# Softmax attentions with two output banks, index scores among slabs, and a residual loaded piece by piece

## The reference

```python
# block 1
h = rms_norm(x); z = h @ w_in                    # glu, q, k, v, two gates
a = silu(rms_norm(causal_depthwise_conv(glu, 31 taps))); y_a = a @ w_conv_out
q, k = rms_norm per head                          # 16 heads of 64
o = sum over 3 dilation groups of softmax(q k' - slope * dist) v   # one merged softmax
y_b = o @ w_attn_out
x = x + (sigmoid(gate_a) * y_a + sigmoid(gate_b) * y_b) @ w_out
x = x + (silu(u_gate) * u_val) @ w_down           # u = 3-tap conv(rms_norm(x) @ w_up)
# layer A: attention over the 128 best keys of an index
score = sum_h relu(qi_h . ki) * wi_h              # 8 index heads
p = softmax(rope(q) rope(k)' over top 128 of score);  y = (p v * silu(g)) @ w_out_a
x = layer_norm(ALPHA * x + y)
# layer B: stick-breaking attention, gate, w_out_b, layer_norm; its result is the output
```

## Time and profile before

| | us |
|---|---|
| median of 3 runs | 1651.69 |
| lowest, highest | 1646.33, 1653.17 |
| the profiled execution | 1649.88 |
| its span | 1648.10 |
| mean granted TensorE clock | 0.984 |

### The profile page before, as it was taken

The page is one execution under the profiler, slowest core; times in us unless marked ns, Lnnn a source line. Parts: engine busy times, 40 slices in busy tenths (PEclk is TensorE's granted clock), DMA queues, the critical chain, the costliest instruction groups (busy, mean ns, idle before and its releaser), DMA issues.

```text
span 1648.1 us, 19418 instructions
## 1 busy us (share of the span) xinstructions
PE 1561.9 (95%) x7634; PEld 1273.9 (77%) x7634; DVE 886.0 (54%) x1546; ACT 504.5 (31%) x1001; POOL 546.1 (33%) x662
## 2 busy tenths in 40 slices
PE   6999999899899999999999999999998989999997
PEld 5878888677778778888878787687776768888885
DVE  2899949256645144333400031895676261677675
ACT  4223333356541132222200011311676130444440
POOL 3222234311114344444444444144110334332321
PEclk9999999999999999999999999999999999999999
DMA  8989998623338978898888888398321758755655
GB/s 227 193 184 194 195 191 188 153 66 63 77 77 183 225 169 193 191 198 190 196 172 192 184 176 194 78 189 182 77 52 26 164 120 193 156 123 117 140 109 145
DMA packets 69274, 253.12 MB, mean 154 GB/s; under 512 B 7616, under 2 KB 7744, under 8 KB 69184
## 3 DMA queue, kind: packets, MB, share of 16 engines
q0 software_dynamic: 66528, 242.25, 68.7%
q1 hardware_dynamic: 2112, 7.53, 1.3%
q10 hardware_dynamic: 544, 2.10, 0.4%
HBM read 249.75 MB, written 2.10 MB: 153 GB/s over the span
## 4 chain that ended last, share of the span: by engine, by line
PE 86%; DVE 5%; DMA 3%; ACT 3%; issue 2%; POOL 0%; SPq 0%; DVEq 0%; ACTq 0%; POOLq 0%
PE PSUM L451 26%; PE PSUM L452 25%; PE PSUM L453 25%; DMA W_LO<-wstream 2%; PE PSUM L612 2%; PE PSUM L633 2%; PE PSUM L714 1%; PE PSUM L732 1%; PE PSUM L745 1%; PE PSUM L600 1%; DVE MASK L1747 1%; DMA SMALLS<-small 1%; DMA W_HI<-wstream 1%; PE PSUM L643 1%; ACT PROBS L968 0%
## 5 line engine op out<-in xcount | busy, mean ns | idle before, releaser
L439 POOL DMA_DIRECT2D W_HI<-wstream x231 | 129.5, 561 | 946.8 <-PE PSUM L453 946.3
L451 PE MATMUL PSUM<-X_HI,W_HI 128*128 128x512 f32 x872 | 350.0, 401 | 5.7 <-DVE X_LO L1332 2.6
L452 PE MATMUL PSUM<-X_LO,W_HI 128*128 128x512 f32 x872 | 342.1, 392 | 0.0
L453 PE MATMUL PSUM<-X_HI,W_LO 128*128 128x512 f32 x872 | 342.0, 392 | 0.0
L433 POOL DMA_DIRECT2D W_LO<-wstream x231 | 208.0, 900 | 105.2 <-POOL W_LO L430 84.2
L451 PE MATMUL PSUM<-W_HI,X_HI 128*128 128x512 f32 x544 | 213.8, 393 | 7.0 <-DMA W_LO<-wstream 2.7
L430 POOL TENSOR_SCALAR W_LO<-W_HI 128x1024 fp32r<-128x1024 f32 x195 | 210.3, 1079 | 23.1 <-DMA W_HI<-wstream 19.6
L452 PE MATMUL PSUM<-W_LO,X_HI 128*128 128x512 f32 x544 | 212.8, 391 | 0.0
L453 PE MATMUL PSUM<-W_HI,X_LO 128*128 128x512 f32 x544 | 212.7, 391 | 0.0
L451 PEld LDWEIGHTS PSUM<-X_HI,W_HI 128*128 128x128 f32 x872 | 165.0, 189 | 44.8 <-issue 7.5
L453 PEld LDWEIGHTS PSUM<-X_HI,W_LO 128*128 128x128 f32 x872 | 164.7, 189 | 35.8
(11 more groups left out here) (225 smaller groups left out, 2465.8 us busy)
## 6 DMA issues: line engine op xcount, KB each, us to landing
W_HI<-wstream POOLq DMA_DIRECT2D x231, 512.0 KB, 3.9
W_LO<-wstream POOLq DMA_DIRECT2D x231, 512.0 KB, 5.7
GATE_A<-x SPq DMA_DIRECT2D x4, 512.0 KB, 5.8
GATE_B<-x SPq DMA_DIRECT2D x1, 2048.0 KB, 16.5
NORM_GAINS<-lnv ACTq DMA_DIRECT2D x2, 1024.0 KB, 5.9
out<-GATE_B SPq DMA_DIRECT2D x3, 512.0 KB, 2.6
CONST<-consts SPq DMA_DIRECT2D x1, 968.0 KB, 10.7
out<-GATE_B SPq DMA_DIRECT2D x2, 256.0 KB, 2.0
```

The source lines that it names most:

```text
L439: pool.dma_start(W_HI[:, n % SLOTS, :], wstream[n]).then_inc(w_hi_in[n % SLOTS], 16)
L451: pe.matmul(o, lh, rh, start=start, stop=False)
L452: pe.matmul(o, lh, rl, start=False, stop=False)
L453: return pe.matmul(o, ll, rh, start=False, stop=stop)
```

## The change

- **Values.** `V_HI` and `V_LO` become two views of one buffer `ATT_V`; each head's products go to a bank of its own (`OUT_BANK` 2 and 3, for the last pair other ones), 16 matmuls. ACT gets `low_products` (two copies of 64 x 512), DVE `both_parts` (two additions of 64 x 512) before `output`. The zeroing of V's other halves goes.
- **Banks and order in the attentions.** Scores have one pair of banks (0 and 1), so each `scores` waits for both `biased` of the one before it. q and k are turned into a bank of their own (7), one at a time: `turn_qk(i+1, 0)` after `turn_inverse(i-1)`, `turn_qk(i+1, 1)` after `values(i-1)`. `turn_p` waits for `pt_lo` of the pair before alone. `scores(i, 3)` moves behind `turn_p(i, 0)` and `(i, 1)`. The fill tables change; every pair of b has one slab, [1, 1, 0, 2]. The two early slabs of b go. `soft_stats` has two halves for the row sums.
- **Ends.** `attention_out` (a) does 7/8 of the first two `attn_out` slabs before it needs the last pair; `out_a` (b) puts the last transposes and values between its own slabs.
- **Index.** The weights are turned after the first slab of `q2`, q and k of the index after the second and third; 4 scores stand before the second half of `q2` and 4 before each of its k = 1 to 5. Both halves of `q2` go to banks 4 to 7.
- **Low parts.** After the last slab of `w_out`, `down` and `out_a`, `remainder` is issued before the next slab's wait.
- **Residual.** x is loaded in 8 pieces of 128 columns into the third part of `QKV`, each when `v_lo` of that pair is done.
- **Banks of first halves.** `qkv` starts in banks 4 to 7, `conv_out` uses them, `early` and `v_tail` use 0 to 3; `down` waits for 4 tiles fewer; so no phase starts in the banks that the one before it just filled.
- **Tables.** The tables of Exp and Sigmoid are loaded ahead by an activation of one element.

```diff
-SCORE_BANK, TURN_BANK, SLAB_BANK, OUT_BANK = ((0, 1), (2, 3)), (4, 5), 6, 7
+SCORE_BANK, OUT_BANK, TURN_BANK, SLAB_BANK, QK_BANK = (0, 1), (2, 3), (4, 5), 6, 7
+FIRST_QK_BANK, FIRST_SLAB_BANK = SCORE_BANK, OUT_BANK[1]
+LAST_OUT_BANK = dict(a=OUT_BANK, b=(SLAB_BANK, QK_BANK))
+INDEX_TURNS = ((TT, 0), (0, 1), (1, 2), (2, 3), (3, 0))
+EARLY_REMAINDER = [SLAB_END[name] - 1 for name in ("w_out", "down", "out_a")]
-A_EARLY, B_EARLY = 4, 2
-A_FILL = 2 * [[2, 2, 0, 2], [2, 0, 2, 2], [0, 2, 2, 0]] + [[2, 2, 0, 2], [2, 0, 0, 0]] + [[4, 4]]
-B_FILL = [[1, 1, 1, 1], [0, 1, 1, 1], [1, 0, 1, 1], [1, 1, 0, 1], [1, 1, 1, 0], [1, 1, 1, 1], [0, 0, 1, 0], [0, 1, 0, 0]] + [[2, 0]]
+A_FILL = [[4, 2, 0, 2]] + 2 * [[2, 2, 0, 2], [2, 2, 0, 2], [1, 1, 0, 2]] + [[1, 1, 0, 2]] + [[2, 2]]
+B_FILL = [[3, 1, 0, 2]] + (PAIRS - 2) * [[1, 1, 0, 2]] + [[1, 1, 0, 0]]
...
-            sp.wait_ge(tile_free, TILE0["attn_out"] + 8)
-            sp.dma_start(RESIDUAL, x.rearrange("(t p) d -> p t d", p=P)).then_inc(sem("res_in"), 16)
+            for k in range(KT):
+                sp.wait_ge(sem("a_v_lo"), k + 1)
+                sp.dma_start(X_AGAIN[:, :, o_part(k)], x[:, o_part(k)].rearrange("(t p) d -> p t d", p=P))\
+                    .then_inc(sem("res_in"), 16)
...
             for n in range(SLABS):
+                if n - 1 in EARLY_REMAINDER:
+                    remainder(n - 1)
                 if n >= SLOTS:
                     pool.wait_ge(slab_done, n - SLOTS + 1)
...
-                if n:
+                if n and n - 1 not in EARLY_REMAINDER:
                     remainder(n - 1)
...
                 def scores(i, q):
-                    after(pe, f"{a}_biased", 2 * (4 * i + q) - 2)
+                    after(pe, f"{a}_biased", 2 * (4 * i + q))
...
                     for h in range(2):
                         for kb in range(TT):
-                            mm = mm3(PSUM[:, OUT_BANK, kb * P:], V_HI[:, kb, h, :], V_LO[:, kb, h, :], ...
+                            for part in (PT_HI, PT_LO):
+                                mm = pe.matmul(PSUM[:, out_bank(a, i)[h], kb * P:], ATT_V[:, kb, h, :],
+                                               part[:, h, r, :].rearrange("p b q -> p (b q)"), ...
...
                 for i in range(PAIRS):
                     scores(i, 0)
                     if i:
                         turn_p(i - 1, 2)
-                    fill(i, 0)
+                    fill(i, 0, slice(0 if i else 2, None))
                     scores(i, 1)
                     if i:
                         turn_p(i - 1, 3)
                         turn_inverse(i - 1)
+                    if i < PAIRS - 1:
+                        turn_qk(i + 1, 0)
                     fill(i, 1)
                     scores(i, 2)
-                    fill(i, 2)
-                    if i < PAIRS - 1:
-                        turn_qk(i + 1)
                     if i:
                         values(i - 1)
-                    scores(i, 3)
+                    if i < PAIRS - 1:
+                        turn_qk(i + 1, 1)
                     turn_p(i, 0)
                     turn_p(i, 1)
+                    scores(i, 3)
                     fill(i, 3)
                 turn_p(PAIRS - 1, 2)
...
+            def out_a(last_scores, last_values, fill):
+                pe.wait_ge(sem("b_biased"), 8 * PAIRS)
+                pe.wait_ge(sem("b_add"), 2 * PAIRS - 2)
+                t_half(0, s0, KT, O_HI, O_LO, TILE0["g2"] + 1, ready, slabs=(0,))
+                last_scores()
+                t_half(0, s0, KT, O_HI, O_LO, TILE0["g2"] + 1, ready, slabs=(1,))
+                last_values()
+                t_half(0, s0, KT, O_HI, O_LO, TILE0["g2"] + 1, ready, slabs=(2, 3))
...
+            t_half(4, s0, KT, X_HI, X_LO, i0 + 4,
+                   aside={1: turn_weights, 2: lambda: turn_index(INDEX_TURNS[:4]), 3: lambda: turn_index(INDEX_TURNS[4:])})
+            index_scores(0)
+            t_half(4, s0 + 4, KT, X_HI, X_LO, t0 + 4, scores_beside)
```

## The result

The changed kernel takes 1572.71 us (median of 4 runs, 1572.17 to 1574.10), the one before 1652.26 beside it: a ratio of 0.9527, 95% interval 0.9504 to 0.9551, 4.7% faster. The forecast was 1566, 6.7 us too low and inside its range. The profiled execution took 1572.18 us, its span 1570.4.

A forecast was written before the change was run, and what follows sets the result against it. PE was taken as the bound, busy 95% of the span, so removed matmuls and PE's waits count. Gains of 83 us from the profiled 1649.9 gave 1567, forecast as 1566 us (5.2% faster), range 1553 to 1590.

The forecast's parts named there:

- The sum: Whole kernel: gains of 39, 25, 7, 4.3, 4.6, 1.5 and 1.7 us add to 83 us.
- Values: Both softmax attentions: a block falls from 3.96 to 2.60 us, 21.8 us over 16 blocks, all on PE.
- PE stays the bound in b: A pair of attention b: PE has 14.75 us, DVE 13.8, ACT 12.7; PE stays longest by 0.9 us.
- the walk: New order stepped through with an attention b pair's times; some 0.3 us to spare at turn_p(i, 2).
- Attention a: Softmax attention a: 43.0 us from waits, clock and values, less 4 returned; net gain 39 us.
- given back, 4: Attention a: loss taken off its gain for head_bias and gates on DVE; 4 us, bounds 0 and 13.
- The new wait of scores(i, q) for `biased(i, q-1)` holds nothing: Attentions: this wait costs nothing, since PE has 2 us or more of other work between two scores.
- DVE as the bound: Rival in the attention pairs: DVE becomes the bound, 1572 to 1594 us, middle 1583; chance 15%.
- Attention b: Softmax attention b: 31.0 us from waits, clock and values, less 6 returned; net gain 25 us.
- Index: Stretch of the index: 9.5 us of waits and half clock, less new costs; 7 us taken, bounds 4 and 9.5.
- the 13.76 us of the scores themselves stay PE work: Index: its scores keep costing PE 13.76 us, now between matmuls of q2, so no gain from them.
- Small parts: Outside attentions and index: first halves 1.7 us, w_out's low part and residual 3.1, down's start and low part 5.8.

The follow-up runs named there:

- dve_more: Changed kernel with one more 128x512 addition on DVE ahead of biased(i, 3) in pairs 1 to 6 of attention b; 1575.94 us.
- index_apart: Changed kernel with all index transposes and all 24 scores placed between the halves of q2, not among its slabs; 1581.82 us.
- wait_back: Changed kernel in which turn_p(i, 0) waits again for both low parts of the next pair's q and k; 1601.06 us.
- fill_moved: Changed kernel with other fill tables in attention a, moving PE's slab quarters in pairs 3, 4, 6 and 7; 1570.37 us.
- both combined ones: Changed kernel with new fill tables in a, b's last-pair order and attn_out's early low part, 1565.92 us; also with head_bias in three half buffers, 1564.49 us.
- values24: Changed kernel with the third matmul of values put back in both softmax attentions, 24 matmuls a block; 1597.66 us.
- down_resid_back: Changed kernel with down waiting for all tiles of up and the residual loaded as one 2 MB transfer, as before; 1578.82 us.

## Why the prediction was right, and where it missed

*The sum.* 83 came to within 6 us of what the profiles show, and that is in part luck: a gained 7.2 us less than forecast, and attn_out, `up` and the end lost 5.2, while the index gave 4.7 more and the other parts 2.0.

*Values.* Right: 2.61 us a block, and 20.9 us back when the products are put back.

*PE stays the bound in b.* Right: pairs of 14.92 for 14.75. DVE was mis-sized: 12.52 us in the pair, not 13.8. The 12.32 taken as its start came from a window of before that held four biased blocks of 384 columns (2.1 us) and two out_lo, where one pair has two and one: 1.8 us too many, against one gate too few. The new v_lo took 0.69 there, not 0.96; only one of the eight in a took 0.97, at 399.49, beside a negation. The margin that counts is not in such a sum: dve_more puts it at 0.2 to 0.3 us, the walk's size, but at scores(i+1, 0) and not where the walk had it.

*Attention a.* The old waits went, as forecast, but the gain is 31.8 for 39. The term "given back, 4" was 8 (7.2 us idle, with the extra of each gap). The step that failed is "The new wait of scores(i, q) for `biased(i, q-1)` holds nothing": 6.0 of the 7.2 us stand at this wait. The walk was one of b; in a head_bias (1.40) and the gate stand in DVE's run, and `output` takes 2.03 us in four of the eight pairs instead of the 0.68 it has in b. I had seen that the gate reads two SBUF operands, but not that `output`, with ATT_LOW in the place of PSUM, does so now: its row begins at 412.00 and POOL's negation runs from 412.41 to 413.47. The Trainium skill, page SBUF — State Buffer, section Who interferes with whom, says that a DVE instruction with two SBUF inputs contends with a GpSimd one that reads SBUF. The trace agrees: the four outputs beside a negation take 2.03 us and the four others 0.68, and the gate at 415.27, behind the negation, takes 0.68, where the earlier trace rows had 1.65 on average. The collision changed its victim: in a gates and outputs took 13.2 + 8 x 0.69 = 18.7 us before and take 8.8 + 10.9 = 19.7 now. The other 3.2 us: a matmul of the filling starts 0.43 us after the one before at half clock and 0.23 at full, so half clock costs a little under half, some 0.7 us of it in a; 2.5 us stay open. The pairs of b, which have no wait, last 0.17 us more than the sum for them, 14.92 for 14.75; if the pairs of a do the same, 1.4 of the 2.5 are that (an estimate).

*"DVE as the bound"*, the rival at 1583, came true in part: in a alone, in and beside the pairs with four quarters, 6.0 us.

*Attention b.* Right: 25.9 for 25. The wait at its end was foreseen at 2.1 with 1.7 of half clock and came as 2.31 with the same. The half clock is luck in part: ten profiles have this wait of 2.31, and seven the half clock with it.

*Index.* Too small: 11.7 for 7, outside the bounds of 4 to 9.5. 8.8 of it lie before kv2 (57.55 us for 66.30) and 2.9 in it, where the kernel before had 6.8 us of half clock. The step that failed is "the 13.76 us of the scores themselves stay PE work". The earlier trace rows show one busy row of 48 matmuls, and in it PE was kept at the pace of ACT's Relu and DVE's sum, one of each for every score. Between slabs the same 48 take 9.0 us: 4.8 gained, as index_apart shows from the other side. 7 + 4.8 = 11.8 is the measured gain. The wait of 1.1 for q2's tiles came as forecast.

*Small parts.* First halves 1.9 for 1.7, w_out 3.6 for 3.1, down 6.2 for 5.8: right. Putting the low parts back costs 6.0 for 4.6, the residual and down 6.1 for 5.8.

*Not in the sum.* attn_out lost 2.6: its first two slabs now end together, so slab 3's low part, queued behind the load that waits for slab 0, comes late. I said that behind the earlier `remainder` only the next slab's issue is queued, and didn't ask which other low parts stand behind such a wait. And a stretch of half clock ahead of `up` (1.7), and 0.9 at the end.

## To carry to other kernels

Take an engine's load per iteration over a full period and not over a window that happens to be free of stalls, and then walk the order, to every wait and above all to the new ones: the margin that decides is that of the longest run without a stop. A row of many matmuls counted as busy can hide waits; divide it by their number and compare with the same shape elsewhere. When an operand moves from PSUM to SBUF, list every instruction that reads it, and time each beside the other engine's work.

## What was unexpected in the hardware

The half clock behind the same waits comes and goes. Ahead of `up` PE waits 0.77 and 0.98 us in each of these kernels, to 0.01 us. In the changed one, wait_back, fill_moved, index_apart and both combined ones (six of thirteen) a stretch of 3.4 us at 0.50 follows within 2 us (548.8:552.2 above), in the other seven none does; it is worth 1.7 us. Attention a of the changed kernel has two waits of 2.0 us and no half clock. Seven of the experiments have the same two waits. In dve_more a stretch follows the first (417.7), in values24 (443.3) and down_resid_back (435.1) the second, in the other four none does. dve_more and down_resid_back change nothing in a, and there a is 1.7 and 1.5 us longer. The wait of 2.31 at b's end has it in seven profiles of ten. Every wait of 2.5 us and more has it, in the kernel before and in all thirteen others, but for the load at the start. So a term for the clock can be taken from rows for a wait of 2.5 us; up to 2.3 us it is a chance.
